# Weaving the first expert's token picks into its own gate and up products

## The reference

```python
g_prob = softmax(xt @ wg + bg)             # 8 groups of 8 experts
g_p, g_idx = top_k(g_prob, 1)              # one group for each token
e_in = take(xt @ we + be, g_idx)           # the 8 experts of that group
e_val, e_loc = top_k(e_in, 2)              # two experts in it
weight = g_p * softmax(e_val)
# for each of the 64 experts, on the tokens that chose it:
y = (silu(xc @ w_gate[e]) * (xc @ w_up[e])) @ w_down[e]
```

## Time and profile before

| | |
|---|---|
| profiled execution | 1948.38 us, its span 1946.6 us, mean granted clock 0.991 |
| median of three runs | 1948.68 us |
| TensorE busy | 1871.2 us, 96% of the span |
| DMA | mean 260 GB/s; from the 21st of 40 slices on 420 to 430 GB/s |
| chain that ended last | TensorE 81%, DMA 16% |

### The profile page before, as it was taken

How to read it: one execution, slowest core, us unless ns; L and a number is a source line. 1 busy time by engine, 2 the same in 40 slices (tenths; PEclk the granted TensorE clock), 3 DMA queues, 4 the chain that set the end, 5 groups by cost and what they waited for, 6 DMA issues and landing times.

```text
span 1946.6 us, 28605 instructions
## 1 busy us (share of the span) xinstructions
PE 1871.2 (96%) x11936; PEld 1352.2 (69%) x11936; DVE 705.6 (36%) x1773; ACT 584.6 (30%) x1212; POOL 245.3 (13%) x208
## 2 busy tenths in 40 slices
PE   6999999999999999999999999989999899999997
PEld 6887777777777767788986666556665565656663
DVE  5331223333766668701042232322323222222222
ACT  5323333333443444422312232212212122121322
POOL 2433343433000000144100000000000000000000
PEclk9999999999999999999999999999999999999999
DMA  9554233234232232145489999999999999999995
GB/s 284 134 147 118 66 86 82 70 71 92 45 76 44 55 117 79 44 142 195 191 349 420 429 426 426 427 427 427 427 426 427 427 428 426 428 427 427 427 423 231
DMA packets 177745, 505.95 MB, mean 260 GB/s; under 512 B 52930, under 2 KB 136258, under 8 KB 151754
## 3 DMA queue, kind: packets, MB, share of 16 engines
q1 hardware_dynamic: 175306, 495.66, 66.5%
q0 software_dynamic: 2304, 8.39, 1.1%
HBM read 495.88 MB, written 16.53 MB: 263 GB/s over the span
## 4 chain that ended last, share of the span: by engine, by line
PE 81%; DMA 16%; ACT 1%; DVE 1%; issue 0%; SPq 0%; POOL 0%; POOLq 0%; ACTq 0%; DVEq 0%
PE banks L967 26%; PE banks L1375 13%; PE banks L1124 9%; PE banks L1400 8%; DMA x_region<-in_w_up 7%; DMA at_region<-in_w_up 7%; PE banks L1297 6%; PE banks L1376 3%; PE banks L1104 3%; PE banks L1076 2%; PE banks L1054 2%; PE banks L1346 2%; DMA ht_region<-in_w_up 2%; PE banks L1016 1%; PE banks L1215 1%; PE banks L1061 1%
## 5 line engine op out<-in xcount | busy, mean ns | idle before, releaser
L967 PE MATMUL banks<-ht_rounded,ring_rounded 128*128 128x512 f32 x1056 | 359.2, 394 | 0.7 <-ACT at_region L1538 0.7
L967 PEld LDWEIGHTS banks<-ht_rounded,ring_rounded 128*128 128x128 f32 x1056 | 195.1, 188 | 53.3 <-issue 13.8
L1375 PE MATMUL banks<-at_region,ht_region 128*64 128x256 f32 x800 | 179.0, 382 | 9.3 <-DMA at_region<-in_w_up 9.3
L864 POOL TENSOR_TENSOR ring_rounded<-ring_region,at_rounded 128x512 fp32r<-128x512 f32 (+1 forms) x92 | 115.9, 1291 | 511.3 <-ACT at_rounded L1477 511.3
L1376 PE MATMUL banks<-at_region,ht_region 128*64 128x256 f32 x768 | 175.3, 388 | 0.0
L2269 DVE SCALAR_TENSOR_TENSOR at_rounded<-banks,small,ring_rounded 128x512 fp32r<-128x512 f32 x128 | 96.1, 751 | 208.8 <-ACT ring_rounded L1763 207.9
L1763 ACT ACTIVATE ring_rounded<-banks,small 128x512 fp32r<-128x512 f32 x128 | 88.0, 687 | 241.3 <-PE banks L1400 241.3
L2262 DVE COPY consts<-banks 128x128 f32<-128x128 f32 x64 | 18.7, 292 | 388.1 <-PE banks L1385 388.1
L1375 PEld LDWEIGHTS banks<-at_region,ht_region 128*64 128x64 f32 x800 | 109.1, 138 | 67.3 <-issue 21.1
L967 PE MATMUL banks<-ht_rounded,at_rounded 128*128 128x512 f32 x352 | 142.7, 405 | 1.0 <-ACT at_region L1530 0.7
L1753 ACT ACTIVATE ring_region<-banks,consts 64x256 f32<-64x256 f32 x64 | 30.0, 469 | 364.4 <-PE banks L1376 364.1
(11 more groups left out here) (300 smaller groups left out, 3488.2 us busy)
## 6 DMA issues: line engine op xcount, KB each, us to landing
at_region<-in_w_gate SPq DMA_DIRECT2D x23, 2048.0 KB, 30.0
at_region<-in_w_up SPq DMA_DIRECT2D x22, 2048.0 KB, 27.6
at_region<-in_w_down SPq DMA_DIRECT2D x22, 2048.0 KB, 23.9
ring_region<-in_w_in SPq DMA_DIRECT2D x36, 1024.0 KB, 5.9
x_region<-in_w_down SPq DMA_DIRECT2D x17, 2048.0 KB, 26.6
x_region<-in_w_up SPq DMA_DIRECT2D x15, 2048.0 KB, 28.9
x_region<-in_w_gate SPq DMA_DIRECT2D x14, 2048.0 KB, 29.9
ring_region<-in_w_gate SPq DMA_DIRECT2D x9, 2048.0 KB, 32.6
```

The lines of the kernel that those rows point to most:

```text
L864: ins = nc.gpsimd.tensor_tensor(w_low[n % RING][:, ks, 0:width], ring[n % RING][:, ks, 0:width], w_high[n % 2][:, ks, 0:width].bitcast(F32 ...
L967: ins = mm(out, w[:, k, 0:width], h[:, k, :], start=k == 0 and i == 0, stop=k == KT - 1 and i == 2)
L1375: mm(place[0:CAP, 0:D_EXPERT], x, gate[j], start=j == 0, stop=j == KT - 1)
```

## The change

It has three parts. SyncE's wait ahead of L798 is for the gather's issue (`g_copied`) and no longer for its landing. Of TensorE's filling products 16 become 7, 4 become 1 and 6 become 2. The 16 picks of experts 0 to 3 are no longer a block: four stand ahead of expert 0's `gate_up`, and each of the first 12 steps of it has one pick ahead of it. The eight tiny products with the norm factors move from its start to its end. VectorE builds `pick` in two halves, and the picks wait for the first. The four banks that the picks go round change, since expert 0's own result needs one of the old ones. The copies keep their order and sizes.

```diff
@@ SyncE
-            sp.wait_ge(xg_in[0], 16)
+            sp.wait_ge(g_copied, 1)
             for k in range(2):
...
                 sp.dma_start(second_gate[k], sources[kind][:, e, half]).then_inc(once_in, 16)
@@ TensorE
             place_rows(0)
-            keep_busy(16)
+            keep_busy(7)
             pe.wait_ge(chosen_ready, 1)
...
             ins.then_inc(ranks_ready, 1)
-            keep_busy(4)
+            keep_busy(1)
             place_slots(0)
-            keep_busy(6)
+            keep_busy(2)
+            def pick_first(part, j):
+                lo, hi = FIRST_PARTS[part]
+                if j == 0:
+                    pe.wait_ge(first_picks, part + 1)
+                if part == 0 and j == 0:
+                    pe.wait_ge(idx_ready, 1)
+                    pe.wait_ge(xg_in[0], 16)
+                places = first_places[part]
+                at = j - len(places)
+                if at >= 0:
+                    pe.wait_ge(xT_v if at % 2 else xT_a, part * KT // 2 + at // 2 + 1)
+                mm(places[j % len(places)][:, 0:hi - lo], first_rows[:, j, :], pick[:, lo:hi], start=True, stop=True).then_inc(picked, 1)
...
-                if e8 == 0:
+                def root_of_slots():
...
+                if e8 == 0 and not begins_all(c, g):
+                    root_of_slots()
                 for j in range(KT):
...
+                    if begins_all(c, g) and e8 == 0 and j + len(first_places[0]) < KT:
+                        pick_first(0, j + len(first_places[0]))
                     x = xT[:, 0 if fast(c) else e8 // 4, j, e8 % 4 * CAP:(e8 % 4 + 1) * CAP]
                     mm(place[0:CAP, 0:D_EXPERT], x, gate[j], start=j == 0, stop=j == KT - 1)
                     ins = mm(place[CAP:2 * CAP, 0:D_EXPERT], x, up[j], start=j == 0, stop=j == KT - 1)
...
+                if e8 == 0 and begins_all(c, g):
+                    pe.wait_ge(pick_ready, 1)
+                    ins = root_of_slots()
                 ins.then_inc(gu_done, 1)
...
-            pick_half(0, 0)
+            for j in range(len(first_places[0])):
+                pick_first(0, j)
@@ VectorE
-            build_pick(0, 0)
+            v.tensor_copy(group_slots, slot_of_row[:, 0:PER]).then_inc(own_slots, 1)
...
+            for lo, hi in FIRST_PARTS:
+                es = slice(lo // CAP, hi // CAP)
+                v.tensor_tensor(pick_by_slots[:, es, :], bcast(iota, 1, es.stop - es.start),
+                                bcast(group_slots[:, es], 2, CAP), ALU.is_equal).then_inc(first_picks, 1)
+            es = slice(HALF // CAP, PER)
+            v.tensor_tensor(pick_by_slots[:, es, :], bcast(iota, 1, PER - es.start), bcast(group_slots[:, es], 2, CAP),
+                            ALU.is_equal).then_inc(pick_ready, 1)
...
-            copy_half(0, 0)
+            copy_first(0)
```

More of the change, by code:

```diff
@@ L1279, in pick_half @@
             def pick_half(g, h):
                 pe.wait_ge(pick_ready, g + 1)
-                pe.wait_ge(idx_ready, 1)
-                pe.wait_ge(xg_in[g % 2], g // 2 * 16 + 16)
-                place, turn = half_places(g, h)
                 rows = xg[g % 2].rearrange("r (p k) -> r k p", k=KT)
+                if not h:
+                    pe.wait_ge(xg_in[g % 2], g // 2 * 16 + 16)
                 for j in range(KT):
-                    if (h or g) and j == TURN4.index(0):
+                    if j == TURN4.index(0):
@@ L1294, in pick_half @@
                     if i is not None:
-                        pe.wait_ge(xT_v if i % 2 else xT_a, copies_ahead(0, g) + h * 8 + i // 2 + 1)
+                        pe.wait_ge(xT_v if i % 2 else xT_a, copies_ahead(0, g) + half_after(g, h) + i // 2 + 1)
                     slots = pick[:, h * HALF:(h + 1) * HALF]
-                    mm(place[turn[j]][:, 0:HALF], rows[:, j, :], slots, start=True, stop=True).then_inc(picked, 1)
+                    mm(whole_banks[TURN4[j]][:, 0:HALF], rows[:, j, :], slots, start=True, stop=True).then_inc(picked, 1)
@@ L1356, in gate_up @@
                 picks = e8 // (PER // 2) if fast(c) and e8 % (PER // 2) == 0 else None
-                done = copies_ahead(c, g) + (picks or 0) * (KT // 2)
+                done = copies_ahead(c, g)
+                if picks:
+                    done += half_after(g, picks)
+                if begins_all(c, g) and any(e8 * CAP == lo for lo, _ in FIRST_PARTS[1:]):
+                    picks, done = -1, KT // 2
                 if e8 == 0 and not fast(c):
@@ L1360, in gate_up @@
                     pe.wait_ge(xT_v, done + 8)
-                if picks is not None:
+                if picks is not None and (g or e8 >= PER // 2):
                     i = max(j for j in range(KT) if TURN4[j] == 1)
@@ L1423, in group @@
                     if begins_all(c, g) and e8 == 0:
+                        for part in range(1, len(FIRST_PARTS)):
+                            for j in range(KT):
+                                pick_first(part, j)
                         place_marks(c)
@@ L1729, in copy_half, with copy_first @@
             def copy_half(g, h):
[L1730 removed]
                 for j in range(0, KT, 2):
[L1732 to L1733 removed]
+                    act.wait_ge(picked, picks_ahead(0, g) + 2 * half_after(g, h) + j + 1)
+                    fn(xT[:, 0, j, :], whole_banks[TURN4[j]][:, 0:HALF], ACT.Copy, scale=ln2_sb[:, j:j + 1]).then_inc(xT_a, 1)
+            def copy_first(part):
+                lo, hi = FIRST_PARTS[part]
+                for j in range(0, KT, 2):
+                    act.wait_ge(picked, part * KT + j + 1)
+                    fn(xT[:, 0, j, lo:hi], first_places[part][j % len(first_places[part])][:, 0:hi - lo], ACT.Copy, scale=ln2_sb[:, j:j + 1]).then_inc(xT_a, 1)
             def square_rows(c, g, b):
@@ L1790, in _ @@
             fn(r_tmp[:, 4], r_tmp[:, 3], ACT.Exp).then_inc(e_exped, 1)
-            copy_half(0, 0)
+            for part in range(len(FIRST_PARTS)):
+                copy_first(part)
             for g in range(N_GROUPS):
```

39 lines of the change are left out of this document (26 added, 13 removed).

## The result

The changed kernel takes 1960.97 us, median of six runs (1958.4 to 1963.28); before it is 1948.14, also of six. The ratio is 1.0061 with a 95% interval of 1.0051 to 1.0071, so the change costs 10 to 14 us: 0.7% at most, but clear of no change. I had forecast 1951.2 and at most 1955.6.

What follows compares the result with a forecast made beforehand. TensorE's arrival at the fifth expert's release was taken to set the end, the weight stream running full after it. Terms -0.8 + 1.2 + 2.0 + 0.1 + 0 = +2.5 us gave 1951.2 us, range 1947.6 to 1955.6.

Steps and rivals of the forecast that it cites:

- What bounds the end: TensorE's release of a place after expert 4's `gate_up`, at 1053.67: the kernel's end is this release plus a constant.
- the rival in which the stream carries its start: L798's load, issued 4.0 us earlier, takes that off the end in full: 1944.7 us; chance 0.06.
- Term 1: Start of the picks: gather lands 1.0 us later, at 985.8, picks start earlier: -0.8 us, bounds -1.8 and +3.3 to +5.8.
- the other alternation: At the gather, engines drain 9 to 17 descriptors from one ring before turning; sum higher by 1.8 to 4.2 us.
- Term 2: TensorE's clock probably low when the picks start, after fewer fillers: +1.2 us, bounds 0 and +3.4 for two stretches.
- Term 3: TensorE waits at `place_marks` for VectorE's marks, since the last pick comes later: +2.0 us, bounds 1.5 to 2.5.
- Term 4: Weaving picks among expert 0's steps, whole-array beside half-array products: +0.1 us, upper bound +1.8.

Runs made afterwards that it cites:

- b_issue: Kernel before with only the last free place's load waiting for the gather's issue, not its landing: 1950.5 us, ratio 1.0012.
- h_tune: Changed kernel with woven picks as half-array products, marks' product behind expert 1's gate and up, wait for gather's landing, fillers 11, 2, 6: 1948.7 us, ratio 0.9996.
- w_block: Changed kernel with the weaving alone undone, all 16 picks a block ahead of expert 0's gate and up: 1951.9 us, ratio 1.0022.
- w_only: Changed kernel with fillers of 16, 4, 6 and the wait for the gather's landing put back: 1956.1 us, ratio 1.0034.
- w_half: Changed kernel with each woven pick of expert 0 issued as two half-array products: 1955.4 us, ratio 1.0031.
- s_block: Kernel before with 12 more picks, read by nobody, in one block ahead of expert 1's gate and up: 1955.2 us, ratio 1.0039.
- s_woven: Kernel before with 12 more picks, read by nobody, one ahead of each of expert 1's first 12 steps: 1960.1 us, ratio 1.0061.
- n_tune: Changed kernel with the picks as a block, the wait for the gather's landing, and fillers of 11, 2 and 6: 1948.6 us, ratio 0.9997.

## Why the prediction was wrong

**What bounds the end: right.** The release moved by 9.2 us from the anchor, the end followed, and the rival in which the stream carries its start is refuted by b_issue and h_tune.

**Term 1: within its bounds, with luck.** Forecast -0.8, measured -0.3. The landing moved by 1.3 us where I had 1.0. In the other kernels with the early load it landed after 6.8 to 8.1, 1.4 to 2.7 later than before, and in w_block the first pick was 1.1 late, so my value was at the low side. The working behind it does not hold. I took 144 records for nine rounds of 8 KB on each engine, but 0.44 MB are only 54 records of 8 KB, 3 or 4 for each. And 16 records beside 20 in one us, summed over 16 engines, do not show the order in which one engine takes them. So they do not speak against the other alternation, with a landing 8.2 to 10.6 us after the issue; the landings of 6.7 to 7.2 us do, and w_block's 8.1 is close to it. The mask was late too: it was ready 4.65 us after `chosen` and not 3.66, since `place_slots` ran at low clock (1.97 us for 1.00), but the gather came later still and hid it.

**Term 2: the mechanism right, the size too small.** I took +1.2 for one low stretch, with +3.4 as the bound for two. In the changed kernel both came: the first picks and the marks' product at 0.50. First pick to release is 9.5 us longer; of this w_only, whose clock was full, explains 7.0, and so 2.4 are the clock's. A count of its own gives nearly that: 2.4 us of low clock in the picks cost 1.2, and the marks' product was 1.6 longer, 2.8 together. Whether the clock is low there varies from execution to execution (last section).

**Term 3: right.** 2.0 forecast, 2.07 in the changed kernel and 2.1 in w_only, to be had from the order and four rows.

**Term 4: the step that failed.** The prediction says of the weaving, the alternation of picks and steps: "In the chain the block of picks, the tiny products and the steps follow one another without a gap, and I take +0.1", and sets the upper bound to 1.8. It is 5.0: 12 visits at 0.42, and w_half, with the same order in one tile shape, has none of it. Two things were wrong in it. The price of a change was read off places where it happens once, and there I had 0.36 against 0.21 in hand and put the 0.15 down to a wait for a copy; s_block shows the same 0.36 with no such wait. And a visit has two changes. The one back, from half-array products to a whole-array weight load, I had no row for, and I left it out of the bound. It is the dearer one: 0.74 - 0.46 = 0.28. "Without a gap" was read from TensorE's products alone; in the trace of before the first half-array weight load behind the picks, at 993.94, has 0.23 us idle in front of it, the same as in the woven pair shown above.

**The signs.** All that I had named as signs came: the landing at 6.7 us, the load at the gather's issue, the low clock at the picks, the wait of 2 us with VectorE's product as releaser, the longer dip. They stood for terms 1 to 3. None was set for the weaving, so they could come true with the sum wrong; the time of one woven pair would have been that sign.

**The sum.** -0.3 + 2.4 + 2.1 + 5.0 = 9.2, what the release shows; the 2.4 is what the others leave over, so the sum is no proof of itself. The medians differ by 12.8, the two profiled spans by 12.4. Of the 3.2 us between 9.2 and 12.4, 2.5 are a later `chosen` and 0.8 the way from the release to the end. They are no edit's that I could find: `chosen` lies anywhere between 980.7 and 983.5 over the fourteen profiles, before at 981.0, and the profile of before had the shortest way from the release to the end. Neither is settled further.

## What to carry to other kernels

Count the changes of tile shape when products of two kinds are woven: a visit of whole-array products among half-array ones cost 0.42 to 0.45 us here, and splitting the visitor into two half-array products took it to nothing. Before booking idle time of a saturated stream as a gain, look for its last drain; here only what moved that moved the end. And when a chain on another engine follows the last of a series, moving that last one later moves the whole chain.

## What was not expected of the hardware

**Weight loads across tile shapes.** In the changed kernel the loads of a pick (128x128) and of a gate product (128x64) start only about when the products of the other shape end, 0.39 and 0.23 us idle in front of them. In w_half all loads are 128x64 and run beside the products. What in the array makes them wait no run here tells.

**The fillers have two speeds.** In s_woven the code up to the picks is that of before. Its clock stayed full where before it was at 0.50, the 16 fillers ended in time for `chosen`, and the first pick came at 4.13 us and not at 5.48:

```profile
978.00:979.00 1.00, 1.00 (x11) 1.00 (x11) 0.93 (x4) 0.00 (x0) 0.00 (x0) 1.00 0.99 426
...
980.00:981.00 1.00, 1.00 (x12) 1.00 (x11) 0.86 (x5) 0.00 (x0) 0.85 (x1) 1.00 1.11 475
```

So an execution of before can be 1.35 us better or worse here by the clock alone, and one profile does not say which it usually is. If it is usually the better one, which is not shown, n_tune's 3.97 is a gain of 0.16 us and not of 1.5, and that its median shows nothing would be no wonder.
